# A hybrid decoder layer on one core: the opening in token halves, and another order of chain steps and weight casts

## The reference

```
h   = concat(meta_tokens, x)                       # 528 x 2048
hn  = rms_norm(h, pre_norm_w)
proj = hn @ w_in                                   # 2048 x 8320 columns
y_r = rwkv7(proj[:, r k v and 128 LoRA columns]) * silu(proj[:, gate])        # 16 heads of 64
y_d = diff_attention(proj[:, q k v])             * silu(proj[:, gate])        # 8 heads of 128
y   = concat(y_r, y_d) @ w_out                     # 2048 x 2048
out = (h + rms_norm(y, post_norm_w))[16:]
```

## Time and profile before

| | us |
|---|---|
| median of 3 runs | 1368.49 (1368.04 to 1368.84) |
| the profiled execution | 1368.25 |
| its span, first to last instruction | 1366.4 |
| PE busy | 1299.5 (95%) |
| DVE busy | 713.9 (52%) |
| ACT busy | 700.2 (51%) |
| POOL busy | 304.7 (22%) |
| granted TensorE clock, mean | 0.996 |

### The profile page before, as it was taken

How to read it: one execution, slowest core, us unless ns; L and a number is a source line. 1 busy time by engine, 2 the same in 40 slices (tenths; PEclk the granted TensorE clock), 3 DMA queues, 4 the chain that set the end, 5 groups by cost and what they waited for, 6 DMA issues and landing times.

```text
span 1366.4 us, 24244 instructions
## 1 busy us (share of the span) xinstructions
PE 1299.5 (95%) x9393; PEld 1107.9 (81%) x9393; DVE 713.9 (52%) x1653; ACT 700.2 (51%) x1670; POOL 304.7 (22%) x234
## 2 busy tenths in 40 slices
PE   3999999999999999999999999999999999999996
PEld 2988788787887879788788788798888988678885
DVE  5346766867577686766866434343343433530013
ACT  4435766566665666666566534344453444442321
POOL 3340001000010100001000333334334343334443
PEclk9999999999999999999999999999999999999998
DMA  6221121111212111121112222222222222226333
GB/s 215 70 80 57 48 58 46 57 53 50 57 48 64 48 55 57 48 57 48 55 49 69 78 70 70 70 70 78 71 77 78 70 77 73 67 93 224 101 97 141
DMA packets 151265, 102.27 MB, mean 75 GB/s; under 512 B 6398, under 2 KB 140640, under 8 KB 149600
## 3 DMA queue, kind: packets, MB, share of 16 engines
q1 hardware_dynamic: 151152, 100.72, 24.7%
HBM read 96.50 MB, written 4.19 MB: 74 GB/s over the span
## 4 chain that ended last, share of the span: by engine, by line
PE 78%; DVE 8%; ACT 8%; issue 4%; POOL 1%; DMA 0%; ACTq 0%; DVEq 0%; SPq 0%
PE tile L569 45%; PE tile L835 2%; PE tile L836 2%; PE tile L837 2%; PE ma L805 2%; ACT arena L1097 2%; PE ma L680 2%; ACT w_hi L932 1%; PE mb L820 1%; PE ma L671 1%; PE ma L712 1%; PE ma L835 1%; PE ma L837 1%; PE ma L836 1%; PE mb L835 1%
## 5 line engine op out<-in xcount | busy, mean ns | idle before, releaser
L569 PE MATMUL tile<-hn_hi,w_hi 128*128 128x264 f32 (+1 forms) x1696 | 445.0, 325 | 0.0
L569 PE MATMUL tile<-hn_hi,w_lo 128*128 128x264 f32 (+1 forms) x1696 | 437.5, 321 | 0.0
L569 PE MATMUL tile<-hn_lo,w_hi 128*128 128x264 f32 (+1 forms) x1696 | 436.6, 320 | 0.0
L932 ACT CAST w_hi<-w_raw 128x512 fp32r<-128x512 f32 x324 | 200.3, 619 | 336.1 <-PE tile L569 231.6
L1243 POOL TENSOR_TENSOR w_lo<-w_raw,w_hi 128x512 fp32r<-128x512 f32 x196 | 254.9, 1302 | 443.0 <-ACT w_hi L932 442.9
L569 PEld LDWEIGHTS tile<-hn_hi,w_hi 128*128 128x128 f32 x1696 | 276.1, 189 | 27.4 <-issue 10.2
L569 PEld LDWEIGHTS tile<-hn_hi,w_lo 128*128 128x128 f32 x1696 | 275.6, 189 | 15.1 <-issue 3.4
L569 PEld LDWEIGHTS tile<-hn_lo,w_hi 128*128 128x128 f32 x1696 | 275.2, 189 | 11.1 <-issue 2.2
L1258 POOL TENSOR_TENSOR arena<-arena,power 128x10 f32<-128x10 f32 (+3 forms) x28 | 44.0, 1570 | 598.5 <-DVE arena L1427 462.4
L1097 ACT ACTIVATE arena<-ma 64x192 f16<-64x192 f32 x240 | 78.0, 325 | 43.1 <-PE ma L671 40.6
L1507 DVE TENSOR_TENSOR w_lo<-w_raw,w_hi 128x512 fp32r<-128x512 f32 x128 | 87.4, 683 | 1.3
(11 more groups left out here) (250 smaller groups left out, 2087.0 us busy)
## 6 DMA issues: line engine op xcount, KB each, us to landing
w_raw<-w_in SPq DMA_DIRECT2D x260, 256.0 KB, 2.9
w_raw<-w_out SPq DMA_DIRECT2D x64, 256.0 KB, 3.0
big<-x SPq DMA_DIRECT2D x4, 1024.0 KB, 7.9
arena<-x SPq DMA_DIRECT2D x4, 1024.0 KB, 8.6
out<-big SPq DMA_DIRECT2D x3, 1024.0 KB, 3.9
arena<-post_norm_w SPq DMA_DIRECT2D x1, 1024.0 KB, 4.9
out<-big SPq DMA_DIRECT2D x2, 512.0 KB, 3.2
arena<-table_rope SPq DMA_DIRECT2D x2, 264.0 KB, 2.8
```

The lines of the kernel that those rows point to most:

```text
L569: last = mm(o[:, at:at + n], w[:, slot, cols], t[:, kt, tok:tok + n], start=(kt == 0 and w is w_hi and t is hn_hi), stop=(kt == KT - 1 and ...
L932: nc.scalar.copy(w_hi[:, slot, :], w_raw[:, slot, :]).then_inc(s("hi_done"), 1)
```

## The change

- **Chain steps:** `CHAIN_FROM` goes from 4.7 to 4.202, so that a chain step on PE is put right behind a step of the inverse; the copies on DVE are due 0.52 steps behind it, those on ACT 0.1 and 1.25. Some copies of the inverse move by 0.05 or 0.1 step.
- **Weight casts:** on ACT they are a generator, due 0.8 places behind the head of a unit; on POOL the subtractions, due at 1.6.
- **514 columns of r:** the r tile is done without its first 14 tokens (the first part has 250 columns).
- **Centred v:** v is turned by a matmul with the centring matrix instead of the identity, so that y needs no centring; L610 and the copy L1008 are gone, the square and the scale read `ysum`.
- **The opening:** meta rows are laid on 128 partitions, squared, summed by a small matmul with a new `group` matrix, and turned once; hn_hi, hn_lo and the LoRA tile are done in 2 x 16 steps, first meta and tokens 0 to 255, then tokens 256 to 511. Constants are loaded in two parts; LoRA units between x tiles. PE does 4 and 20 matmuls on the identity that nobody reads (`keep_clock`).
- **Attention** starts at other places in iterations 9 to 11, and iteration 10 too hands over what is late. **The output** has two features split ahead, and waits for the gate tile only at the rows that use its bank.

```diff
-FULL = {"rwkv": (True, True, True, False), "attn": (False, True, True, False)}
+FIRST = {"rwkv": (0, 0, META - 2, None), "attn": (None, 0, 0, None)}
...
-        CHAIN_FROM, CHAIN_STEP = 4.7, 1.0
+        CHAIN_FROM, CHAIN_STEP = 4.202, 1.0
...
-        PADS_AT = (46.2, 48.1, 49.2, 51.25)
+        PADS_AT = (46.2, 47.6, 48.9, 50.3)
...
         def attn_stage_at(i):
-            return {FIRST_ATTN: 12, FIRST_ATTN + 1: 8.4}.get(i, 0)
+            return {FIRST_ATTN: 12, FIRST_ATTN + 1: 12.4, FIRST_ATTN + 2: 4.8}.get(i, 0)
         def attn_at(i, qi):
-            start, step = {FIRST_ATTN: (21.8, 12.0), FIRST_ATTN + 1: (11.5, 12.4)}.get(i, (6.5, 13.0))
-            return start + step * qi
+            return {FIRST_ATTN: 22.4, FIRST_ATTN + 1: 14.8, FIRST_ATTN + 2: 8}.get(i, 6.5) + 13 * qi
...
         def y_split_at(k):
-            return max(4 * k - 7, -1) if k < KT - 1 else 200
+            return 60.4 + 1.6 * k if k < AHEAD_Y else max(4 * k - 7, -1) if k < KT - 1 else 200
...
+            sp.dma_start(xm, meta_tokens.rearrange("r (k c) -> (r k) c", c=MW)).then_inc(s("meta_in"), 16)
+            sp.dma_start(c32[:, 0:2 * P], c32_dram[:, 0:2 * P]).then_inc(s("ident_in"), 16)
+            load_x(0)
+            load_x(1)
...
+            load_lora(0)
+            load_x(2)
+            load_lora(1)
+            load_x(3)
+            for h in range(2, UPT):
+                load_lora(h)
+            sp.dma_start(c32[:, 2 * P:], c32_dram[:, 2 * P:]).then_inc(s("const_in"), 16)
...
+            def lora_part(j):
+                part, k = divmod(j, KT)
+                at, tok, n = ((512 - FIRST_HALF, 0, FIRST_HALF), (512, FIRST_HALF, L - FIRST_HALF))[part]
+                h, c = divmod(k, UK)
+                cols = slice(c * P, (c + 1) * P)
+                pe.wait_ge(s("hn_lo_made"), j + 1)
+                pe.wait_ge(s("lo_done"), h + 1)
+                for n_, (w, t) in enumerate(((w_hi, hn_hi), (w_hi, hn_lo), (w_lo, hn_hi))):
+                    last = mm(tiles[0][:, at:at + n], w[:, h, cols], t[:, k, tok:tok + n],
+                              start=(k == 0 and n_ == 0), stop=(k == KT - 1 and n_ == 2))
...
+            keep_clock(4)
+            pe.wait_ge(s("norm_sq"), 1)
+            mm(mb[:, 0:1], c32v("group"), norm_s[:, 4:5], start=True, stop=True).then_inc(s("meta_summed"), 1)
+            keep_clock(WARM)
...
+            for j in range(2 * KT + LORA_LAG):
+                if j < 2 * KT:
+                    part, k = divmod(j, KT)
+                    if j >= 4:
+                        pe.wait_ge(s("hn_lo_made"), j - 3)
+                    for t in (2 * part, 2 * part + 1):
+                        if k in (0, KT // 2):
+                            pe.wait_ge(s(f"x_scaled{t}"), 1 if k == 0 else 2)
+                        last = nc.tensor.transpose(turn_home(j)[:, t % 2 * P:(t % 2 + 1) * P],
+                                                   xin[:, t, k * P:(k + 1) * P], ident)
+                    last.then_inc(s("x_turned"), 1)
+                if j == LORA_LAG:
+                    pe.wait_ge(s("meta_lo"), 1)
+                if j >= LORA_LAG:
+                    lora_part(j - LORA_LAG)
...
-                mm(o[:, 0:SEQ], c32v("centre"), ysum, start=True, stop=True).then_inc(s("centre_done"), 1)
-                yield gn_at(work) + 4
-                pe.wait_ge(s("centre_taken"), n * 2)
+                pe.wait_ge(s("y_squared"), n)
...
-                            last = nc.tensor.transpose(bank(1, c), xv[:, ch * CH:(ch + 2) * CH], ident)
+                            last = mm(bank(1, c), xv[:, ch * CH:(ch + 2) * CH], c32v("centre"), start=True, stop=True)
...
+                    if n + k + t == 0:
+                        pe.wait_ge(s("tile_freed"), N_TILES)
...
+            square_sum(4, 0)
+            square_sum(0, 1)
+            square_sum(1, 2, slice(0, D // 2))
+            split_hi(0, 0, 1)
+            square_sum(2, 3)
+            act.wait_ge(s("meta_by_pre"), 1)
...
-                A(t512, gn_home(work)[:, 0:SEQ], ACT.Copy).then_inc(s("centre_taken"), 1)
-                A(t512b, gn_home(work)[:, 0:SEQ], ACT.Square).then_inc(s("centre_taken"), 1)
+                A(t512b, ysum, ACT.Square).then_inc(s("y_squared"), 1)
...
+            def weights_act(i):
+                for k in range(KT):
+                    yield k * UK + 0.8
+                    if i or k:
+                        split_hi(unit_of(i, k + AHEAD), (k + AHEAD) % RING, i * 4 + (2 + (k + AHEAD) // UPT))
...
-                for k in range(16):
-                    if i or k:
-                        split_hi(unit_of(i, k + AHEAD), (k + AHEAD) % RING, i * 4 + (2 + (k + AHEAD) // UPT))
-                    upto(gens, k * UK + 3)
+                gens += begin(weights_act(i))
```

More of the change, by code:

```diff
@@ L96, in constants @@
     causal = np.where(t <= s, 0.0, NEG).astype(np.float32)
-    f32 = np.concatenate([ident, masks, centre, block, heads, heads / HD, causal], 1).astype(np.float32)
+    group = (s // (P // META) == t // (P // META)).astype(np.float32)
+    f32 = np.concatenate([ident, group, masks, centre, block, heads, heads / HD, causal], 1).astype(np.float32)
     levels = [ident]
@@ L118 @@
 _n = 0
-for _name, _w in (("ident", P), ("masks", 2 * CH), ("centre", P), ("block", P),
+for _name, _w in (("ident", P), ("group", P), ("masks", 2 * CH), ("centre", P), ("block", P),
                   ("heads", 2), ("heads_mean", 2), ("causal", P)):
@@ L572, in feature_tile @@
                 return last
-            pe.wait_ge(s("const_in"), 16)
[L575 to L598, removed]
@@ new lines, in keep_clock @@
+            def keep_clock(count):
+                for _ in range(count):
+                    mm(tiles[0][:, 512:512 + P], ident, ident, start=True, stop=True)
+            def lora_part(j):
[8 more added lines that the diff above has]
+                              start=(k == 0 and n_ == 0), stop=(k == KT - 1 and n_ == 2))
+                if part and c == UK - 1:
+                    last.then_inc(s("unit_used"), 1)
@@ new lines, in _ @@
+            for m in range(2):
+                last = nc.tensor.transpose(tiles[1][:, m * P:(m + 1) * P], xm[:, m * P:(m + 1) * P], ident)
+            last.then_inc(s("meta_turned"), 1)
+            pe.wait_ge(s("par_made"), 1)
+            for j in range(2 * KT + LORA_LAG):
[13 more added lines that the diff above has]
+                    lora_part(j - LORA_LAG)
@@ L868, in body @@
                     upto(gens, -1)
-                    pe.wait_ge(s("tile_freed"), N_TILES)
-                    for k in range(KT - 1):
+                    out_feature(0, 0, gens, rows=(2, 3, 0, 1))
+                    for k in range(1, KT - 1):
                         out_feature(0, k, gens)
@@ L959, in _ @@
             act.wait_ge(s("zeroed"), 1)
-            A(lora[:, PAD:TP], tiles[0][:, EDGE:EDGE + L], ACT.Copy, scale=om_mu[:, 24:25]).then_inc(s("lora_base"), 1)
+            at = 512 - FIRST_HALF
+            A(lora[:, PAD:TP], tiles[0][:, at:at + L], ACT.Copy, scale=om_mu[:, 24:25]).then_inc(s("lora_base"), 1)
             act.wait_ge(s("tile_freed"), 1)
@@ L1136, in chain_act @@
                         last.then_inc(s("s_scaled"), 1)
-                    yield chain_at(g, 3 * c + 1.3, late, work)
+                    yield chain_at(g, 3 * c + 1.25, late, work)
                     if 0 < ch < SC:
@@ L1286, in body @@
                 late.clear()
-                for k in range(16):
-                    if work == "attn" and proj is not None and gn and k == 0:
-                        split_lo_behind(unit_of(i, k + AHEAD), (k + AHEAD) % RING)
-                    elif work != "rwkv":
-                        split_lo(unit_of(i, k + AHEAD), (k + AHEAD) % RING)
-                    upto(gens, k * UK + 3)
-                if i == FIRST_ATTN:
+                gens += begin(weights_pool(i, proj, work, gn))
+                if i in (FIRST_ATTN, FIRST_ATTN + 1):
+                    upto(gens, KT * UK - 0.5)
                     late.extend(carried(g) for g in gens if g[1] is not None)
@@ L1685, in attn_dve, with split_y_dve @@
                 STT(mixed(i - 1), gate2[:], gate_sub[:], ma[:, 0:SEQ], ALU.mult, ALU.mult).then_inc(s("o_made"), 1)
-            def split_y_dve():
-                for k in range(KT):
+            def split_y_dve(features):
+                for k in features:
                     yield y_split_at(k) + 0.1
```

237 lines of the change are left out of this document (137 added, 100 removed).

## The result

The changed kernel takes **1370.99 us** (median of 20 runs, 1367.66 to 1376.55), the kernel before 1368.41 beside it (20 runs, 1367.71 to 1369.18): ratio 1.0018, 95% interval [1.0011, 1.0026]. It is slower by 2.6 us, where 1326.6 was predicted, and the time lies outside the range. The profiled execution took 1368.84 us, its span 1367.1.

What follows compares the result with a forecast made beforehand. PE, busy 95% of the span, bounds the kernel, so it must work or wait less. Savings 10.0 + 4.7 + 14 + 6.4 + 3.5 + 3.3 = 41.9 from 1368.25, plus 0.24, give 1326.6 us; range 1308 to 1350.

Steps and rivals of the forecast that it cites:

- Chain steps behind the inverse's: RWKV iterations: chain matmuls issued right after the inverse's save 6.4 us (0 to 10); the added wait is covered.
- Block adjacency: PE in RWKV iterations: 0.03 to 0.05 us saved where f16 and f32 blocks meet, 27 per iteration.
- rival B: Queues stay full: moved casts delay other copies as much, block order saves PE nothing; 1347 us, chance 0.16.
- Casts in order of places: ACT and DVE queues in RWKV iterations: casts due 0.8 places after a unit's head cut PE's waits; 14 us less (0 to 25).
- Work that PE no longer does: RWKV iterations: centre matmul gone, v by f32 matmuls, fewer r columns; together 4.7 us less (0 to 7).
- The opening: Before iteration 0: PE starts with tokens 0 to 255, ending at 39.5 instead of 49.4; 10.0 us less.
- PE's slow start: Opening: 2.9 us added because PE's first transposes and matmuls take nearly twice their later times.
- Attention's start: Change to attention around iterations 9 and 10: later first blocks and moved stages remove two of four waits; 3.5 us less.
- Output's start: Start of the output: features 0 and 1 split early, rows 2 and 3 need no gate; 3.3 us less.
- rival D: Slower: copies stacked behind each other come late, 0.3 us per chain step, 61 us in all; 1387 us, chance 0.04.
- G: Order in the queues does not change in effect and the rest cancels: no change, 1368 us; chance 0.02.
- what would show me wrong in the main: Steady RWKV iteration staying above 81 us, or PE's waits for DVE (L1596, L1611) and L1601 growing.

Runs made afterwards that it cites:

- dve_copies_old: Changed kernel with only DVE's copies of the chain and of the inverse due where the kernel before has them: 1369.42 us.
- act_copies_old: Changed kernel with only ACT's share of the chain and of the inverse due where the kernel before has it: 1347.45 us.
- copies_old: Changed kernel with the copies of both ACT and DVE due where the kernel before has them, PE's chain steps as changed: 1340.37 us.
- u_lower_behind: Changed kernel with one ACT instruction, the copy of u's lower half, due 0.8 of a step behind PE's u instead of 0.25: 1349.22 us.
- best1: Changed kernel with the whole chain at its old places and, from iteration 9 on, casts at the head of their units: 1325.01 us.
- old_casts: Changed kernel with weight casts (ACT) and subtractions (POOL) at the head of each unit again: 1405.43 us.
- old_both: Changed kernel with chain, casts and the other moved places (pads, x tiles) as before, the rest new: 1348.86 us.
- opening_only: Kernel before with the new opening alone, everything else as before: 1357.42 us.
- casts_earlier: Changed kernel with weight casts due 0.1 instead of 0.8 places behind the head of a unit, chain untouched: 1354.58 us.
- old_chain: Changed kernel with the chain's places (PE steps and copies) as before, casts as changed: 1329.22 us.

## Why the prediction was wrong, point by point

**Chain steps behind the inverse's: the step that failed.** Forecast -6.4 and "covered"; measured +41.8. The prediction followed one wait, PE to DVE's g copy and back, found 1.3 us of 1.785, and closed there. It did not ask its own question, what is queued behind a waiting instruction, for **ACT's** copies. (Its 0.2 us for a signal came from no row, and does not explain the error: in the changed kernel L1168 ends at 353.30 and L750 starts at 353.35.) The diff has them at 0.1 and 1.25, that is, in ACT's queue ahead of the inverse's copies, the cast and the v copies. The u copy there is the worst: it is 0.22 us of work whose data come after PE's u. Moving PE's chain half a step forward moved the copies forward as well, past things that PE needs sooner. In parts, by the kernels in turn: u's lower copy 21.8, ACT's other places 1.8, DVE's on top of them 7.1, PE's own place 11.2.

Part of these sums is the clock: see the last section. DVE's 7.1 us, which are not there when ACT's copies stay as changed (`dve_copies_old` gains 1.6), are mostly that: the steady iteration is 81.9 us in act_copies_old and 80.5 in copies_old, and the one run of act_copies_old with a mean clock of 0.993, not 0.985 to 0.987, took 1340.69, as copies_old does. The 1.8 us of ACT's other places are too small for the same reason: the profiled execution of act_copies_old has five falls of the clock in its RWKV iterations, that of u_lower_behind two.

**Block adjacency gave nothing.** In the chain of waits of copies_old, an f16 block with a chain step right behind it and the projection matmuls after them:

```profile
338.52 0.11 PE ma L756 x3
338.62 0.17 PE ma L726 x3
338.79 0.28 PE mb L815 x2
339.07 0.98 PE tile L604 x8
```

And in best1, the same with four projection matmuls between:

```profile
332.83 0.10 PE ma L750 x3
332.93 0.17 PE ma L720 x3
333.10 0.55 PE tile L598 x4
333.65 0.22 PE mb L809 x2
333.87 0.48 PE tile L598 x4
```

Joined: 0.11 + 0.17 + 0.28 + 0.98 = 1.54 us. Apart: 0.10 + 0.17 + 0.55 + 0.22 + 0.48 = 1.52. The projection matmuls behind the second block are faster, as forecast, but the chain's f32 matmuls take 0.28 instead of 0.22 directly behind f16 ones. The forecast had read 0.03 for this from L691, a block of three; it is 0.06 for a block of two, and nothing is left; in this rival B was right. What the rest of the 11.2 us is, the waits show in part (copies_old has PE waits of 3.0 us in 8 for DVE's state and 4.5 in 7 for L1165, best1 0.5 and 1.9); it was not taken apart further.

**Casts in order of places.** Forecast -14. With the chain at its old places, 1348.86 - 1329.22 = **19.6 us** (it includes the x tiles' and pads' places). The mechanism is the one forecast, and it was undersized: in best1 PE waits for ACT's copies 1.9 us in 8 and 1.8 in 9, where the earlier trace rows had 15.1 in 43, so three quarters went, not 55%. The full stretch beside the v copies, which was to keep 0.9 us an iteration, keeps 0.34. The pads' wait (L1650) is what is left, and larger than before. With the new chain the casts alone were worth 34.4 us (old_casts against after).

**Work that PE no longer does.** Iterations 1 to 8 take 642.9 us in old_both against 647.7: -4.8, against -4.7. The centred v costs more than forecast: by starts two of its matmuls take 0.44 us where two transposes took 0.17 (the 0.25 of the earlier trace rows is one pair behind a wait), 0.13 each instead of the 0.09 to 0.11 forecast. The sum is right.

**The opening.** -11.0 by the changed kernel's trace, -10.0 by that of opening_only, against -10.0. Right. The 2.9 us for PE's slow start were well sized: five steps took 1.1 us each instead of 0.6, 2.6 us; the fast steps are 0.58, not 0.66.

**Attention's start.** Forecast -3.5. Iterations 9 to 12 take 65.2 + 59.2 + 60.2 + 56.9 = 241.5 us against 241.2: nothing. The waits went from iteration 10 to iteration 11. With casts at the head they are 62.1 + 57.8 + 63.9 + 57.2 = 241.0 in best1: again only moved, with 2.4 us in one wait of PE for DVE and the granted clock at the lower level behind it (from 892.3). With casts 0.1 places behind the head, in casts_earlier, they are 63.0 + 57.8 + 60.2 + 56.9 = 237.9, 3.3 less than before: there the forecast was met. So the gain hangs on where the casts stand; what the new places alone bring was not taken apart.

**Output's start.** Forecast -3.3. The gap before the first output matmul is gone and the granted clock is 1.00 in 1164 to 1166, both as forecast; only 1.7 us are won, since L861 waits 1.5 us twice for DVE behind moved casts (3.0 us in 2 waits). With those casts at the head it is 205.2 - 201.0 = 4.2 (best1).

**The sum.** Without the chain's term the forecast was 41.9 - 6.4 = 35.5 less; old_chain is 39.5 less. That they lie so close is in part luck: the casts brought 5.6 us more than forecast, attention and output 5.1 less. The steady iteration of best1 is 78.6 us, where "78.5 to 79" was forecast. So all depended on one term. In mechanism rival D was the closest: its 61 us for "0.3 a step", and its point of decision, 0.2 a step, is met: 41.8 us over its 27 chain steps in 7.5 iterations are 0.21 each. It had 0.04 of the chances, because the slack was taken on DVE, where there was some. By the number G (1368) was nearer, but only because 39.5 and 41.8 cancel; its reason, that the order in the queues does not change in effect, is false. Of "what would show me wrong in the main", the first came true, the iteration above 81; the second did not, since PE's wait for DVE's g copy fell from 4.0 us in all to 0.2 (L1675); and the prediction named no sign on ACT's chain copy at all.

## What to carry to other kernels

When a group of steps is moved in one queue, write down for each engine what the moved instruction now stands ahead of, and when its own data come: an instruction of 0.2 us that reaches the head of an in-order queue too early blocks all that is ready behind it. Move producer and consumers separately, and put the consumer behind everything that is ready sooner and is needed sooner; here that one place was worth 21.8 us of 1371. A small gain forecast from adjacency (6 us) is no reason to accept a change of order in queues whose delays were not each worked out.

## What the runs showed of the hardware that was not expected

**The granted clock can fall behind a short wait, inside a PE that is busy.** act_copies_old loses 1.4 us in five of its six steady iterations against copies_old (81.9 against 80.5). Its PE around 454 us, timeline and then stretches (length, busy, granted clock):

```profile
452.52 0.33 PE L726 MATMUL ma<-c,arena 128*128 128x128 f16 x3
453.14 0.49 PE L820 MATMUL mb<-arena 128*128 128x128 f32 x2 [0.30 <-DVE arena L1686]
453.47 0.39 PE L823 MATMUL mb<-arena 128*128 128x128 f32 x2
453.79 0.40 PE L690 MATMUL tile<-lora,arena 64*128 64x16 f32 x4
454.11 0.61 PE L693 MATMUL tile<-c,arena 128*128 128x2 f32 x4
```

```profile
452.00:454.00 2.00, 1.70 (x19) 1.00 0.07 21
454.00:456.00 2.00, 2.00 (x18) 0.84 0.37 110
456.00:458.00 2.00, 2.00 (x12) 0.50 0.08 24
```

PE waits (0.30 by the view, 0.46 by starts), does a few f32 matmuls, and then fourteen very small ones (16 and 2 columns). From 455 the granted clock is at the 1.2 GHz level for some 3 us, with PE recorded busy all the time. So this place costs about 1.9 us, 0.46 of waiting and 1.4 at the lower level. In copies_old the same wait is 0.25 us by starts and the clock stays at 1.00 in all six steady iterations. But the wait alone does not decide: the first steady iteration of act_copies_old (80.3 us) has the same 0.46 at 209.0 and no fall behind it, and u_lower_behind, with 0.34 there, has a fall in two of its six (82.6 us instead of 81.1). What decides is not shown, and that the small matmuls are a condition was not tried.

**The changed kernel's times spread more than before's:** 1367.66 to 1376.55 against 1367.71 to 1369.18. The mean granted clock goes with it: 0.994 in the fastest run, 0.987 in the slowest, 0.996 in those before. Where the longer executions lose it isn't known, since the profiled one is among the shortest; the candidates are such falls in the iterations and the opening, whose granted clock from 15 to 20 and 20 to 25 us is 0.65 and 0.66 here, 0.54 and 0.50 in copies_old.
